# RWKV factors made ahead: decay sums and keys of all tokens before the chunks, the other factors one chunk early

## The reference

```python
w_log = -softplus(-(w0 + tanh(wd) @ w2)) - 0.5;  decay = exp(-exp(w_log))
a = sigmoid(a0 + ad @ a2)
kk = heads(k * rw_kk);  kk = kk / max(norm(kk, per head), 1e-12)
k = k * (1.0 + (a - 1.0) * rw_ka)
def step(S, inp):                       # over the tokens
    r_t, w_t, k_t, v_t, a_t, b_t = inp  # a_t = -kk, b_t = kk * a
    sa = einsum('bhvk,bhk->bhv', S, a_t)
    S = S * w_t[:, :, None, :] + sa[..., None] * b_t[:, :, None, :] + v_t[..., None] * k_t[:, :, None, :]
    return S, einsum('bhvk,bhk->bhv', S, r_t)
bonus = sum(r * k * rw_rk, axis=-1) * v
```

## Time and profile before

| what | value |
|---|---|
| median of 3 runs | 2142.13 us (2136.95 to 2145.76) |
| the profiled execution, its time | 2145.92 us |
| its span, first to last instruction | 2144.1 us |
| PE busy | 1970.9 us (92%) |
| DVE busy | 1000.6 us (47%) |
| ACT busy | 672.8 us (31%) |
| POOL busy | 73.5 us (3%) |
| granted TensorE clock, mean | 0.94 |
| RWKV stage, from the first chunk's scans to the last `y` | about 366.8 to 546.7 us |

### The profile page before, as it was taken

The page is one execution under the profiler, slowest core; times in us unless marked ns, Lnnn a source line. Parts: engine busy times, 40 slices in busy tenths (PEclk is TensorE's granted clock), DMA queues, the critical chain, the costliest instruction groups (busy, mean ns, idle before and its releaser), DMA issues.

```text
span 2144.1 us, 39908 instructions
## 1 busy us (share of the span) xinstructions
PE 1970.9 (92%) x16899; PEld 1803.4 (84%) x16899; DVE 1000.6 (47%) x1493; ACT 672.8 (31%) x928; POOL 73.5 (3%) x82
## 2 busy tenths in 40 slices
PE   8988887888597999999899999999999799999989
PEld 7967775777275999999899976666999699999978
DVE  6547662555604432343266655555642543244244
ACT  4222214233113332332242123335432342233222
POOL 0000000111000000000100000000001000000000
PEclk9989986899688999999999999999999899999999
DMA  5302101000220222222313234544322122222221
GB/s 197 97 30 79 40 22 42 3 2 3 101 101 29 88 89 88 95 92 89 108 50 118 91 105 166 197 158 176 101 97 88 49 89 89 94 92 88 91 96 60
DMA packets 44751, 187.01 MB, mean 87 GB/s; under 512 B 5481, under 2 KB 5993, under 8 KB 39273
## 3 DMA queue, kind: packets, MB, share of 16 engines
q1 hardware_dynamic: 44648, 185.53, 25.2%
HBM read 160.48 MB, written 25.03 MB: 87 GB/s over the span
## 4 chain that ended last, share of the span: by engine, by line
PE 85%; DVE 10%; ACT 3%; issue 2%; DMA 0%; POOL 0%; POOLq 0%; DVEq 0%; SPq 0%; ACTq 0%
PE ps L2136 52%; PE ps L2019 7%; PE ps L1681 3%; PE ps L332 3%; PE ps L727 3%; PE ps L2084 1%; DVE h_a L1909 1%; PE ps L2094 1%; PE ps L2078 1%; PE ps L350 1%; DVE free L414 1%; PE ps L1705 1%; PE ps L1667 1%; PE ps L2074 1%; DVE rb L369 1%
## 5 line engine op out<-in xcount | busy, mean ns | idle before, releaser
L2124 DVE TENSOR_TENSOR w_low<-slot,w_high 128x1024 fp32r<-128x1024 f32 x240 | 293.5, 1224 | 495.4 <-ACT w_high L2120 495.3
L2120 ACT ACTIVATE w_high<-slot 128x1024 fp32r<-128x1024 f32 x240 | 254.0, 1060 | 800.6 <-PE ps L2136 708.1
L2136 PE MATMUL ps<-x_high,w_high 128*128 128x260 f32 x1600 | 322.7, 283 | 0.4 <-issue 0.4
L2136 PE MATMUL ps<-x_high,w_low 128*128 128x260 f32 x1600 | 322.4, 283 | 0.0
L2136 PE MATMUL ps<-x_low,w_high 128*128 128x260 f32 x1600 | 321.9, 283 | 0.0
L2136 PE MATMUL ps<-hidden_high,w_low 128*128 128x260 f32 x1536 | 309.5, 283 | 0.0
L2136 PE MATMUL ps<-hidden_high,w_high 128*128 128x260 f32 x1536 | 309.4, 283 | 0.0
L2136 PE MATMUL ps<-hidden_low,w_high 128*128 128x260 f32 x1536 | 309.0, 283 | 0.0
L2136 PEld LDWEIGHTS ps<-x_high,w_high 128*128 128x128 f32 x1600 | 247.2, 189 | 1.1 <-issue 0.8
L2136 PEld LDWEIGHTS ps<-x_high,w_low 128*128 128x128 f32 x1600 | 246.7, 188 | 0.0
L2136 PEld LDWEIGHTS ps<-x_low,w_high 128*128 128x128 f32 x1600 | 245.9, 188 | 0.0
(11 more groups left out here) (555 smaller groups left out, 2633.5 us busy)
## 6 DMA issues: line engine op xcount, KB each, us to landing
slot<-in_w SPq DMA_DIRECT2D x240, 512.0 KB, 3.9
h_a<-in_rst SPq DMA_DIRECT2D x16, 1024.0 KB, 5.0
out_rst_o<-h_a SPq DMA_DIRECT2D x16, 1024.0 KB, 3.9
slot<-in_w SPq DMA_DIRECT2D x2, 2048.0 KB, 8.4
h_a<-in_x SPq DMA_DIRECT2D x4, 520.0 KB, 5.3
h_a<-in_x SPq DMA_DIRECT2D x1, 2080.0 KB, 7.7
out_y<-h_a SPq DMA_DIRECT2D x8, 260.0 KB
con<-in_con SPq DMA_DIRECT2D x1, 2062.0 KB, 15.9
```

What stands on the lines that cost most here:

```text
L2120: nc.scalar.activation(wh[c % 2], raw[c % 4], ACT.Copy).then_inc(s_wh, 1)
L2124: nc.vector.tensor_tensor(wl[c % 2], raw[c % 4], wh[c % 2].bitcast(F32), ALU.subtract).then_inc(s_wl, 1)
L2136: mm = pe.matmul(ps[:, 2 * par + hf, 0:HALF], w[c % 2][:, at], y(kt, hf), start=(start and kt == 0 and w is wh and y is x), stop=(stop and ...
```

## The change

Once for all tokens, beside the loras: the decay sums are scanned in place in `sig` (`cumulate`), ScalarE makes the key factor of each head group (in `factor`, behind each gate copy), VectorE mixes all keys in place in `ua`, PE spreads the reciprocal norms over four banks, VectorE normalises all keys (`kkr`) and turns `aa` into kk*a, and GpSimd makes the bonus input of all tokens in `bon_all`. The rest of a chunk's factors is made one chunk ahead: the exponentials (`decays`) before the `bk` copy, `at`, `bt`, `kt` (`keys_and_removals`) between `t8t` and `t16`, `rt` (`receptance`) behind `qp`. The buffer of p is doubled, q gets one of its own. A chunk has 13 rounds instead of 16 and begins with `gram_b`.

```diff
-RW_STAGES = 16
+RW_STAGES = 13
@@ dve_rwkv
+                def keys_and_removals(g):
+                    dve.wait_ge(*ya.at("q", g))
+                    v.scalar_tensor_tensor(by_sub(b.AR[:, 0]), by_sub(th(kkr, h, g)), -1.0, b.pm[g % 2], ALU.mult,
+                                           ALU.mult).then_inc(*yd.step("at"))
+                    v.tensor_tensor(b.bt, th(aa, h, g), b.qq, ALU.mult).then_inc(*yd.step("bt"))
+                    v.tensor_tensor(b.kt, uah(4, h, g), b.qq, ALU.mult).then_inc(*yd.step("kt"))
+
+                def receptance(g):
+                    v.tensor_tensor(by_sub(b.AR[:, 1]), by_sub(uah(0, h, g)), b.pp[g % 2],
+                                    ALU.mult).then_inc(*yd.step("rt"))
+                keys_and_removals(0)
+                receptance(0)
                 for g in range(NG):
...
-                    for j in range(2):
-                        v.tensor_tensor_scan(b.cum[:, j, :], C("reset"), sig[:, 2 * h + j, at], 0.0,
-                                             ALU.mult, ALU.add).then_inc(*rd.step(f"cum{j}"))
-                    yield
...
+                    if g < NG - 1:
+                        after(rp, "bk")
+                        keys_and_removals(g + 1)
                     yield
                     after(ra, "t8")
...
+                    if g < NG - 1:
+                        after(rd, "qp")
+                        receptance(g + 1)
                     yield
...
-            dve.wait_ge(s_one, 3)
+            for ones in rows_of_ones:
+                v.memset(ones, 1.0).then_inc(s_one, 1)
+            dve.wait_ge(s_one, 5)
+            dve.wait_ge(*keyed.at("kka", 3))
             in_rounds(half)
@@ act_rwkv
+                def decays(g):
+                    cum = sig[:, 2 * h:2 * h + 2, L * g:L * g + L]
+                    a.activation(b.pp[g % 2], by_sub(cum), ACT.Exp, scale=-C0).then_inc(*ready_a[h].step("p"))
+                    if g:
+                        act.wait_ge(*ready_d[h].at("kt", g - 1))
+                    a.activation(b.qq, cum, ACT.Exp, scale=C0).then_inc(*ready_a[h].step("q"))
+                decays(0)
...
-            act.wait_ge(s_one, 3)
+            act.wait_ge(s_one, 5)
+            act.wait_ge(s_cum, 4 * NG)
@@ pool_rwkv
+            for j in range(4):
+                pool.wait_ge(s_kp, j + 1)
+                nc.gpsimd.tensor_tensor(bon_all[:, j, :], ua[:, j, 1:TP + 1], ua[:, 4 + j, 1:TP + 1],
+                                        ALU.mult).then_inc(s_bin, 1)
+                pool.wait_ge(s_bin, 2 * j + 1)
+                nc.gpsimd.tensor_scalar(bon_all[:, j, :], bon_all[:, j, :], V("rk", j), None,
+                                        ALU.mult).then_inc(s_bin, 1)
@@ pe_rwkv
-                    after(rd, "kt")
+                    after(ready_d[h], "rt")
@@ dve_tiles
+            for j in range(3):
+                cumulate(j)
             dve.wait_ge(s_kkp, 1)
             v.tensor_scalar(rn, ps[:, 0, 0:32], 1e-24, None, ALU.max).then_inc(s_kk, 1)
             dve.wait_ge(s_kka, 5)
             v.reciprocal(rn, rn).then_inc(s_kk, 1)
+            cumulate(3)
+            for j in range(4):
+                dve.wait_ge(s_tb, j + 1)
+                v.tensor_tensor(ua[:, 4 + j, 1:TP + 1], ua[:, 4 + j, 1:TP + 1], factor[j][:, 0:TP],
+                                ALU.mult).then_inc(s_kp, 1)
+            for j in range(4):
+                dve.wait_ge(s_kn, j + 1)
+                v.tensor_tensor(kkr[:, j, :], kkr[:, j, :], ps[:, j, :], ALU.mult).then_inc(*keyed.step("kkn"))
+                dve.wait_ge(*keyed.at("kkn", j))
+                v.tensor_tensor(aa[:, j, 0:TP], aa[:, j, 0:TP], kkr[:, j, :], ALU.mult).then_inc(*keyed.step("kka"))
@@ act_tiles
                     a.activation(two(gg[:, j, :]), src, ACT.Copy).then_inc(s_lc, 1)
+                    a.activation(factor[j][:, 0:TP], aa[:, j, 0:TP], ACT.Identity, scale=V("ka", j),
+                                 bias=omka[:, j:j + 1]).then_inc(s_tb, 1)
```

More of the change, by code:

```diff
@@ L190 @@
 FFN_CHUNKS = [CHUNKS["up0a"], CHUNKS["up1a"]]
-RW_DVE = ["cum0", "cum1", "kkn", "kp", "rt", "at", "kka", "bt", "kt", "ddd", "bon", "d2t", "t1", "me", "d4t", "t2",
+RW_DVE = ["ddd", "bon", "d2t", "t1", "me", "d4t", "t2",
           "e8t", "t4", "t8t", "t16", "tt", "qp", "sh0", "x0", "mid", "sh1", "x1", "end", "y"]
-RW_ACT = ["p", "q", "tb", "raw", "d2", "d4", "av", "bk", "t8", "mv", "z", "zz", "w", "gh", "yd"]
-RW_POOL = ["rk", "rkw", "nn"]
-RW_PE = ["kn", "gram_b", "bonus", "d2", "gram_k", "d4", "t2", "av", "d8t", "t4", "bk", "t8", "mv", "z", "t16", "zz",
+RW_ACT = ["raw", "d2", "d4", "av", "bk", "t8", "mv", "z", "zz", "w", "gh", "yd"]
+RW_POOL = ["nn"]
+RW_PE = ["gram_b", "bonus", "d2", "gram_k", "d4", "t2", "av", "d8t", "t4", "bk", "t8", "mv", "z", "t16", "zz",
          "tt", "w", "gh", "yd", "s0", "s1"]
-RW_STAGES = 16
+RW_STAGES = 13
 RW_LAG = 0
@@ L638, in after @@
                         act.wait_ge(*steps.at(name, g))
-                    after(rd, "cum1")
-                    a.activation(b.pp, by_sub(b.cum), ACT.Exp, scale=-C0).then_inc(*ra.step("p"))
-                    a.activation(b.qq, b.cum, ACT.Exp, scale=C0).then_inc(*ra.step("q"))
-                    for j in range(2):
-                        put = a.activation(b.tb[:, j, :], aa[:, 2 * h + j, L * g:L * g + L], ACT.Identity,
-                                           scale=V("ka", 2 * h + j), bias=omka[:, 2 * h + j:2 * h + j + 1])
-                    put.then_inc(*ra.step("tb"))
-                    yield
-                    yield
-                    yield
                     after(rd, "ddd")
@@ L662, in half @@
                     yield
+                    if g < NG - 1:
+                        if g:
+                            act.wait_ge(*rd.at("end", g - 1))
+                        decays(g + 1)
                     after(rp, "bk")
@@ L760, in half @@
                     mm.then_inc(*rp.step("gram_b"))
-                    after(rl, "rkw")
-                    pe.matmul(ps[:, Y, 0:256], C("ones64"), b.rkb, start=True, stop=True).then_inc(*rp.step("bonus"))
+                    pe.wait_ge(s_bin, 4 * h + 4)
+                    pe.matmul(ps[:, Y, 0:256], C("ones64"), th(bon_all, h, g), start=True,
+                              stop=True).then_inc(*rp.step("bonus"))
                     yield
@@ L1435, in program @@
         acc = [sqr[0], sqr[1]]
+        factor = [tmp[0], tmp[1], sqr[0], sqr[1]]
         RD = ["i", "ib", "f", "fb", "abs", "lf", "zero", "b", "c", "m", "nm", "nmt", "mo", "t", "tm", "iw", "wi",
```

70 lines of the change are left out of this document (26 added, 44 removed).

## The result

The changed kernel takes 2132.66 us (median of 20 runs, 2125.97 to 2145.46) against 2142.06 for the kernel before (20 runs, 2136.95 to 2151.10): a ratio of 0.9958, 95% interval 0.9948 to 0.9967, that is 7 to 11 us less. Forecast were 18 less (2124, range 2115 to 2134). The time lies in the range, the gain is half of the forecast one, and the time is above the 2131.4 that the prediction had named as the bound of "faster", with a chance of 0.80. Single executions of one kernel differ by more than this gain: 2126 to 2145 for the changed one.

What follows compares the result with a forecast made beforehand. The prediction took TensorE's 26.1 us of waits at `gram_b` for VectorE's factor chain as the bound. Boundaries -23.5, clock -7.0 and setup +11.6 gave -18.9, or -18.1 with the clock kept at two of three: 2124 us, range 2115 to 2134.

Steps and rivals of the forecast that it cites:

- Boundaries, -23.5: At three chunk boundaries `gram_b` starts where `kn` stood, net 7.85 us each, 23.5 us saved.
- clock, -7.0: Full clock kept at two or three of three chunk starts, 3.1 us each, 7.0 us saved, bounds 0 and 9.3.
- Six early ops at nothing: `at`, `bt`, `kt` of both halves fit into idle time before `t16` with 0.2 us to spare, priced at nothing.
- Setup, +11.6: Preparation ahead of chunk 0: `gram_b` 8.3 us later, half 1 another 2.8, clock 0.5; loss 11.6 us (9 to 14).
- scales over 2 us: Named sign of being wrong: GpSimd's one-input scales in the setup, assumed at 0.76 us, taking over 2 us.
- 4.1 sum: Setup from the last `kka` to half 0's `gram_b`: memsets, Exp table, exponentials and four factors, put at 4.1 us.
- B: Rival: clock lost at all or nearly all boundaries and chunk 0's half 1 late, 2128 to 2133 us; chance 0.18.
- The stage as a whole: Sum of boundary gain, clock gain and setup loss: 18.9 us saved.
- outside the RWKV stage it moves nothing that is late: Claim that the change acts only on waits in the RWKV stage; no term for other stages.
- C: Rival: GpSimd and VectorE don't block each other, or the scale is short, and clock kept three times, 2118 us; chance 0.12.
- D: Rival: GpSimd's per-partition scale is slow, deciding at some 6 us more each; about 2151 us at 10 each; chance 0.04.
- E: Rival: another wait fills the freed boundary, half the boundary gain is lost, no change, 2142 us; chance 0.04.

Runs made afterwards that it cites:

- d1: The kernel before, no edit, one more execution with a profile: 2142.22 us (1 run).
- d3: The kernel before, no edit, a third profile: 2140.01 us (1 run).
- c4: The changed kernel with GpSimd's eight bonus operations held back until the last `kka`: 2125.88 us (1 run).
- a4: As a3, with all scans and key products ahead of the reciprocal and each key factor behind its group's sigmoid: 2120.64 us, 0.9903 of before.
- a3: The changed kernel with both halves' chunk 0 factors issued before half 0's first answer and memsets ahead of the scans: 2122.05 us, 0.9913 of before.
- b1: The kernel before with a 1.3 us pause of repeated work behind the last `y`: 2146.60 us, 1.0021 of before.
- b4: a3 with a 1.0 us pause of repeated work behind the last `y`: 2121.76 us, 0.9903 of before.
- c1: The kernel before with unread TensorE products from the last `y` through the one-token recurrence: 2136.56 us, 0.9975 of before.
- c2: The changed kernel with the same unread TensorE products as c1: 2124.43 us, 0.9929 of before.
- b2: The changed kernel with a 2.0 us pause of repeated work behind its last `y`: 2129.19 us, 0.9934 of before.
- c3: a4 with the same unread TensorE products as c1: 2111.68 us, 0.9851 of before.

## Why the prediction was wrong

**Boundaries, -23.5, and clock, -7.0: right.** Chunk by chunk the period of half 0 fell by 8.93, 10.31 and 10.71 us, 29.9 for the 30.5 forecast. The clock fell at the first boundary, for a shorter time, and was kept at two: "two or three of three". The first state step of half 0 began 0.80 us behind `qp` for 0.34, the 0.47 forecast. Before's chunks vary with the clock, too: d1 and d3 had 168.3 and 168.6 us of chunks where the first profile had 170.9, so against those two the same periods save 28.7.

**Six early ops at nothing: right.** `t16` of half 0 has 0.23 us of idle before it in each of the three chunks, the 0.2 that were left.

**Setup, +11.6: right.** Reciprocal to `gram_b` 16.1, forecast 384.1 less 367.97, also 16.1; ACT's part 1.8 for 1.5; chunk 0 from `gram_b` to `y` of half 0 39.77 for 36.08, 3.7 more where half 1 and the clock were put at 3.3; half 1's `gram_b` 5.95 after half 0's for 5.5. Together 12.3. The pieces of it missed a little against each other: the last `kka` ended 11.4 behind the reciprocal's start for 11.9. GpSimd's scale (L718) took 1.88 to 2.40 where 0.76 was put, so the sign of being wrong that the prediction had named, scales over 2 us, came for two of four, and yet VectorE was held up for the 2.1 that c4 shows, near the 2.3 forecast. (Two slips of its arithmetic move nothing: the pieces of its 4.1 sum to 4.0, and B's far end with 3 us is 2136, where the range ends at 2134.)

**The stage as a whole: right.** 12.3 - 29.9 is -17.6, forecast -18.9. On the mean of three profiles of before and four of the changed kernel it is 207.1 against 190.5, -16.6.

**The step that failed** is a sentence, not a term: "outside the RWKV stage it moves nothing that is late". The sum took the 1597 us behind the last `y` as unchanged. They are not: they took 9.3 us longer in the changed kernel (mean of four profiles 1606.5, of three 1597.2), at the same instructions and the same work of the other engines, at a lower granted clock. -16.6 + 9.3 is -7.3, and the medians say -9. The clock was in the prediction, but only as a price at the boundaries; that its changes meet the later work at other places once that work is shifted was not. What the runs showed in its place is two things. The norm stage and the first part of what follows go with the place at which the clock returns: a4 against a3 shows 5.9 us of it, b1 and b4 against before and a3 2.0 and 2.4, all with retention the same to 0.8; c1 and c2, with TensorE busy through the norm stage, bring both kernels' norm stages to 52. And one VectorE product in retention starts 0.35 us later with the changed kernel's queue, behind which the clock falls once more: 4.2 to 4.5 us between profiles that meet the clock at the same places. b2, 2 us of useless work between the stages, takes both away.

**The rivals.** B had the right time (2128 to 2133) for a wrong reason: the clock wasn't lost at the boundaries. C's, that engines don't block each other, falls by c4; D's slow scale was slow by 1.1 to 1.6 us, not by 6; E's wait didn't come. That the forecast range held the time is luck: an error of 9 us in stages that the sum left out fitted within it.

**What stays open.** Why the VectorE product starts 0.35 us late in the changed kernel: it goes with VectorE's queue (six of six profiles, none of twelve others), its releaser was through at the same place, and no run tested more; the link to the third fall in retention rests on pairs of profiles and not on an edit of that product. What a given shift costs in retention and in the stage ahead of it, which the profiles show and nothing here predicts. And some 2 to 4 us between the stages of the profiles and the medians, in c1 and c2 above all: each variant but two has one profile, of one execution out of a spread of 5 to 20 us.

## What to carry to other kernels

A gain in one stage is a gain of the kernel only if the stages behind it take as long as before, so cut both traces into the same stages to the end, and compare granted clock and PE busy time at equal counts of instructions. Where idle stretches of TensorE follow the edited stage, forecast the later stages with a margin (here 0 to 10 us, half of the gain), and don't judge an edit by less than that: a pause of 2 us won about 5, and an edit worth 7 in its stage (a4 over a3) brought 1. When two profiles meet the clock at the same places, align them instruction by instruction: the first start that differs (here by 0.35 us) is where to look, and an added instruction can shift more than time. When work is hoisted ahead of a loop whose halves share in-order queues, issue both halves' first work before either half's answer, and let what has its inputs early run ahead of the last wait: a3 and a4 took the setup's loss back, and with TensorE kept busy (c3) the kernel ran at 2111.68 us, 0.9851 of before.
